# Up-projection of a decoder block by seven half-size products instead of eight, with the second pair's second product between the first pair's fifth and third

## What is computed

```
h = h + merged @ w_out
hn = rms_norm(h, ffn_norm_w)
up = causal_depthwise_conv(hn @ w_up, ffn_conv_w, ffn_conv_b)   # 3 taps
a, gt = split(up, 2)
h = h + (silu(gt) * a) @ w_down
```

## Time and profile before

| | us |
|---|---|
| median of 3 runs (2016.22 to 2018.52) | 2017.21 |
| the profiled execution's own time | 2021.11 |
| its span, first to last instruction | 2019.3 |
| TensorE busy | 1982.7 (98%) |
| VectorE busy | 953.9 (47%) |
| ScalarE busy | 673.2 (33%) |
| mean granted clock | 0.994 |

### The profile page before, as it was taken

One profiled execution on the slowest core, in us unless ns is written; L12 is line 12 of the kernel. 1 busy time (PEld: TensorE's weight loads), 2 busy tenths in 40 slices (PEclk: granted clock), 3 DMA queues, 4 the chain that ended last, 5 costly groups with the idle time before them and its releaser, 6 DMA issues.

```text
span 2019.3 us, 24049 instructions
## 1 busy us (share of the span) xinstructions
PE 1982.7 (98%) x9377; PEld 1698.6 (84%) x9377; DVE 953.9 (47%) x1199; ACT 673.2 (33%) x1179; POOL 98.4 (5%) x153
## 2 busy tenths in 40 slices
PE   6999999999999989999999999999999999999999
PEld 5888999999998877878887878788888888888887
DVE  5534532533443866995326252544344344343433
ACT  6323422432342254114325031433333323232232
POOL 1101110110100000001000010000000000000000
PEclk9999999999999998999999999999999999999999
DMA  6211211111122101210106132211112111022212
GB/s 239 95 52 38 71 61 42 47 50 42 42 69 100 42 1 42 63 42 22 63 22 189 43 113 96 105 42 42 42 46 79 42 42 42 10 84 88 94 47 73
DMA packets 84250, 129.24 MB, mean 64 GB/s; under 512 B 13705, under 2 KB 38281, under 8 KB 84169
## 3 DMA queue, kind: packets, MB, share of 16 engines
q1 hardware_dynamic: 76105, 117.53, 17.8%
q10 hardware_dynamic: 8064, 10.59, 1.5%
HBM read 111.20 MB, written 16.89 MB: 63 GB/s over the span
## 4 chain that ended last, share of the span: by engine, by line
PE 88%; DVE 7%; ACT 2%; DMA 1%; issue 1%; SPq 1%; POOL 0%; ACTq 0%; DVEq 0%
PE psum L248 28%; PE psum L250 28%; PE psum L249 28%; DVE acc L857 2%; DVE acc_odd L857 2%; PE psum L503 1%; DVE wlo L203 1%; PE psum L938 1%; PE psum L359 1%; ACT x_sc L997 1%; DMA x_rows<-in_x 1%; DVE softstat L1084 0%; DVE x_pt_lo L1093 0%; DMA grp<-group_out 0%; ACT x_sc L1012 0%
## 5 line engine op out<-in xcount | busy, mean ns | idle before, releaser
L248 PE MATMUL psum<-act_hi,wlo 128*128 128x512 f32 x1216 | 478.8, 394 | 1.3 <-DVE wlo L203 1.3
L250 PE MATMUL psum<-act_hi,whi 128*128 128x512 f32 x1216 | 474.6, 390 | 0.0
L249 PE MATMUL psum<-act_lo,whi 128*128 128x512 f32 x1216 | 474.5, 390 | 0.0
L248 PE MATMUL psum<-whi,act_lo 128*128 128x512 f32 x768 | 315.0, 410 | 3.0 <-DVE act_lo L1439 2.4
L250 PE MATMUL psum<-whi,act_hi 128*128 128x512 f32 x768 | 305.0, 397 | 0.0
L249 PE MATMUL psum<-wlo,act_hi 128*128 128x512 f32 x768 | 305.0, 397 | 0.0
L250 PEld LDWEIGHTS psum<-act_hi,whi 128*128 128x128 f32 x1216 | 228.9, 188 | 48.0
L248 PEld LDWEIGHTS psum<-act_hi,wlo 128*128 128x128 f32 x1216 | 229.1, 188 | 47.4 <-issue 1.4
L249 PEld LDWEIGHTS psum<-act_lo,whi 128*128 128x128 f32 x1216 | 229.1, 188 | 46.1
L198 ACT CAST whi<-stage 128x512 fp32r<-128x512 f32 x290 | 175.2, 621 | 256.7 <-PE psum L250 244.4
L203 DVE TENSOR_TENSOR wlo<-stage,whi 128x512 fp32r<-128x512 f32 x290 | 189.7, 688 | 118.8 <-ACT whi L198 117.9
(11 more groups left out here) (198 smaller groups left out, 2476.6 us busy)
## 6 DMA issues: line engine op xcount, KB each, us to landing
stage<-in_w_in SPq DMA_DIRECT2D x144, 256.0 KB, 4.1
stage<-in_w_up SPq DMA_DIRECT2D x88, 256.0 KB, 4.0
stage<-in_w_down SPq DMA_DIRECT2D x44, 256.0 KB, 2.6
group_out<-ob ACTq DMA_DIRECT2D x24, 256.0 KB, 2.1
grp<-group_out SPq DMA_DIRECT2D x24, 256.0 KB, 3.2
stage<-in_w_mem_kv SPq DMA_DIRECT2D x16, 256.0 KB, 8.7
x_rows<-in_x SPq DMA_DIRECT2D x2, 2048.0 KB, 13.5
stage<-in_w_out SPq DMA_DIRECT2D x16, 256.0 KB, 7.1
```

The costliest lines, as they stand in the source:

```text
L248: nc.tensor.matmul(dst, lhs[1], rhs[0], start=first, stop=False, skip_group_check=True)
L249: nc.tensor.matmul(dst, lhs[0], rhs[1], start=False, stop=False, skip_group_check=True)
L250: return nc.tensor.matmul(dst, lhs[0], rhs[0], start=False, stop=last, skip_group_check=True)
```

## The change

The up-projection of a pair is a 2 x 2 block product: gate and value columns by the two halves of the depth, and the two halves of the depth by the two halves of the tokens. The change computes it by Strassen's scheme in Winograd's form: 7 products of 4 depths x 512 tokens (12 matmuls each) instead of 8. Products 1, 2, 3 use plain blocks of weights or activations, the others use sums of them:

- Activations: four differences T1 to T4 of blocks, made once at the entry by VectorE from raw transposed rows `xt` (copied by ScalarE, no longer split from PSUM), then split like all operands (`t_act_hi`, `t_dve_lo`).
- Weights: for each pair four sums (`up_dve_sum`) on VectorE, seven high parts (`up_act_hi`) on ScalarE and seven low parts (`up_dve_lo`) on VectorE. The raw weights of a pair come by two DMAs of 512 KB (`up_load`).
- Results: products 1, 6, 5, 3 add into one PSUM bank, and ScalarE copies it between them (`s1`, `q1`, `q2`, `c12`); 2 has a bank, 7 and 4 share one. VectorE adds `c11`, `c22`, `c21` into `yg` and `yv` in SBUF; the taps are made from there.
- SBUF holds no `gated` any more during the stage: each pair's result goes to DRAM (`up_store`) and returns in `down_stage` (`load_gated`), pieces 8 to 21 first.
- TensorE's order in a pair is 6, 7, 5, then 1 of the next pair, 3, 4, then 2 of the next pair. At the entry: 1 and 2 of pair 0, 1 of pair 1 (from weights held in `u_next`), the last transposes, 6, 7, 5 of pair 0, 2 of pair 1, 3, 4. `u_next` lies on the bytes of `u_sums`. Batch 2 of the rows is transposed within tile 7 of `w_out_stage`.
- The first down pieces are split after the last pair is complete on both engines.

```diff
-N_UP = NU // 2
-BASE_DOWN = BASE_UP + N_UP * RING
+BASE_DOWN = BASE_UP
...
+        HALF_K = KT // 2
+        xt = [at(f"xt{b}", FREE + off, [KT, HB]) for b, off in enumerate((86016, 0, 8192, 16384))]
+        T_BYTES = HALF_K * CW * 4
+        t2, t3, t4 = ([at(f"t{n}_{part}", (2 * i + j) * T_BYTES, [HALF_K, CW], F32R)
...
+        moving = {1: b11, 2: b21, 3: b22, 4: t4, 5: t1, 6: t2, 7: t3}
...
+        u_raw = [at(f"u_raw{par}", U_W + par * 8192, [2, KT, P]) for par in range(2)]
+        u_hi = at("u_hi", U_W + 16384, [7, HALF_K, P], F32R)
+        u_lo = at("u_lo", U_W + 16384 + 14336, [7, HALF_K, P], F32R)
+        u_sums = at("u_sums", U_W + 45056, [4, HALF_K, P])
+        u_next = [at("u_next_hi", U_W + 45056, [2, HALF_K, P], F32R),
+                  at("u_next_lo", U_W + 45056 + 4096, [2, HALF_K, P], F32R)]
+        yg = at("yg", FREE, [S])
...
+        gated_dram = nc.dram_tensor("gated_scratch", (NU * P, S), F32).ap()
...
+        BANK_A, BANK_B, BANK_E = (0, 4), (1, 5), (2, 3)
...
+        H_PARTS = [(0, K1), (0, K2), (1, K1), (1, K2), (2, K2), (3, K2)]
+        def h_act_hi(act, which):
+            for n in which:
+                b, k = H_PARTS[n]
+                act.wait_ge(h_raw, (b + 1) * KT)
+                nc.scalar.copy(act_hi[:, k, h_cols(b)], xt[b][:, k, :]).then_inc(h_hi, 1)
...
+        T_SUMS = [(i, q) for q in range(2) for i in (1, 2, 3, 4)]
+        T_HALVES = [(2, 0), (3, 0), (1, 0), (4, 0), (2, 1), (3, 1), (1, 1), (4, 1)]
...
+            near, far = xt[q], xt[q + 2]
+            if i == 1:
+                dve.wait_ge(h_raw, (q + 3) * KT)
+                a, b = far[:, K1, :], near[:, K1, :]
+            elif i == 2:
+                dve.wait_ge(t_sum, T_SUMS.index((1, q)) + 1)
+                a, b = far[:, K2, :], t_raw(1, q)
+            elif i == 3:
+                a, b = far[:, K2, :], far[:, K1, :]
+            else:
+                dve.wait_ge(t_sum, T_SUMS.index((2, q)) + 1)
+                a, b = xt[q][:, K2, :], t_raw(2, q)
+            nc.vector.tensor_tensor(t_raw(i, q), a, b, ALU.subtract).then_inc(t_sum, 1)
...
+        up_cols = w_up.rearrange("(k p) (h c) -> p h k c", p=P, h=2)
+        def up_load(sp, U, par):
+            if not (isinstance(U, int) and U < 2):
+                sp.wait_ge(up_lo[4], U - 1)
+            for kind in range(2):
+                sp.dma_start(u_raw[par][:, kind], up_cols[:, kind, :, bass.ds(U * P, P)]).then_inc(raw_loaded[par], 16)
...
+        S_OF = {5: 0, 6: 1, 7: 2, 3: 3}
...
+        def up_act_hi(act, U, half_U, par, i, ahead=False):
+            first = isinstance(U, int) and U == 0
+            if i in S_OF:
+                act.wait_ge(up_sum, 4 * U + S_OF[i] + 1)
+            else:
+                act.wait_ge(raw_loaded[par], 32 * half_U + 32)
+            if ahead:
+                for n in S_OF:
+                    act.wait_ge(up_lo[n], 1)
+            elif not first:
+                act.wait_ge(up_p[i], U)
+            nc.scalar.copy(up_slot(i, 0, ahead), up_source(par, i)).then_inc(up_hi[i], 1)
...
+            if s == 0:
+                dve.wait_ge(raw_loaded[par], 32 * half_U + 32)
+                if isinstance(U, int) and U == 1:
+                    dve.wait_ge(up_p[1], 2)
+                    dve.wait_ge(up_p[2], 2)
+                ins = nc.vector.tensor_tensor(u_sums[:, 0], value_low, up_block(par, 4), ALU.add)
+            elif s == 1:
+                dve.wait_ge(up_sum, 4 * U + 1)
+                ins = nc.vector.tensor_tensor(u_sums[:, 1], u_sums[:, 0], up_block(par, 1), ALU.subtract)
+            elif s == 2:
+                ins = nc.vector.tensor_tensor(u_sums[:, 2], up_block(par, 1), value_low, ALU.subtract)
+            else:
+                dve.wait_ge(up_sum, 4 * U + 2)
+                ins = nc.vector.tensor_tensor(u_sums[:, 3], up_block(par, 2), u_sums[:, 1], ALU.subtract)
+            ins.then_inc(up_sum, 1)
...
+        def up_q2(act, U, par):
+            first = isinstance(U, int) and U == 0
+            act.wait_ge(up_p[5], U + 1)
+            if not first:
+                act.wait_ge(c22_done, U)
+            nc.scalar.copy(q2[:], psum[:, BANK_A[par], :]).then_inc(q2_done, 1)
...
+        def up_c22(dve, U, par):
+            dve.wait_ge(up_p[7], U + 1)
+            dve.wait_ge(q2_done, U + 1)
+            if not (isinstance(U, int) and U == 0):
+                dve.wait_ge(tap_v, 2 * U)
+            nc.vector.tensor_tensor(yv[:, N2], psum[:, BANK_E[par], :], q2[:], ALU.add).then_inc(c22_done, 1)
...
+        def up_mul(pe, U, par, i, ahead=False, between=None):
+            pe.wait_ge(up_lo[i], U + 1)
+            bank = (BANK_B if i == 2 else BANK_E if i in (7, 4) else BANK_A)[par]
+            for k in range(HALF_K):
+                mm = three(pe, psum[:, bank, :], [up_slot(i, part, ahead)[:, k, :] for part in range(2)],
+                           [half[:, k, :] for half in moving[i]], k == 0 and i in (1, 2, 7), k == HALF_K - 1)
+                if k == HALF_K - 1:
+                    mm.then_inc(up_p[i], 1)
+                if between:
+                    between(k)
...
+        def up_pe_3(pe, U, par):
+            pe.wait_ge(q2_done, U + 1)
+            up_mul(pe, U, par, 3)
...
+                        if j == 1 and t == 7:
+                            def between(k):
+                                if k == 4:
+                                    pe.wait_ge(row_scaled, hr.tile0 + 3 * H_BATCH)
+                                if k >= 4:
+                                    h_pe_bank(pe, 2, 2 * k - 8)
+                                    h_pe_bank(pe, 2, 2 * k - 7)
...
+            def middle(pe, U, par):
+                up_pe_6(pe, U, par)
+                up_pe_7(pe, U, par)
+                up_pe_5(pe, U, par)
+                up_pe_1(pe, U + 1, 1 - par)
+                up_pe_3(pe, U, par)
+                up_pe_4(pe, U, par)
+                up_pe_2(pe, U + 1, 1 - par)
...
+                pe.wait_ge(h_lo, 3)
+                up_pe_1(pe, 0, 0)
+                pe.wait_ge(gemm_freed, io + 2 * NT)
+                pe.wait_ge(h_lo, 4)
+                up_pe_2(pe, 0, 0)
+                pe.wait_ge(row_ss, hr.tile0 + NT)
+                up_pe_1(pe, 1, 1, True)
+                pe.wait_ge(row_scaled, hr.tile0 + NT)
+                for k in range(KT):
+                    h_pe_bank(pe, 3, k)
+                pe.wait_ge(t_lo, T_HALVES.index((2, 1)) + 1)
+                up_pe_6(pe, 0, 0)
+                pe.wait_ge(t_lo, T_HALVES.index((3, 1)) + 1)
+                up_pe_7(pe, 0, 0)
+                pe.wait_ge(t_lo, T_HALVES.index((1, 1)) + 1)
+                up_pe_5(pe, 0, 0)
+                up_pe_2(pe, 1, 1, True)
+                pe.wait_ge(h_lo, 6)
+                up_pe_3(pe, 0, 0)
+                pe.wait_ge(t_lo, T_HALVES.index((4, 1)) + 1)
+                up_pe_4(pe, 0, 0)
+                for U in (1, 2):
+                    middle(pe, U, U % 2)
+                with pe.Fori(1, NU // 2 - 1) as cc:
...
+            def pair_act(act, U, half_U, half_next, par):
+                np = 1 - par
+                start = isinstance(U, int) and U == 0
+                last = isinstance(U, int) and U == LAST
+                if not start:
+                    if not last:
+                        up_act_hi(act, U + 1, half_next, np, 1)
+                    up_silu(act, U - 1, np)
+                up_q1(act, U, par)
+                if not last:
+                    up_act_hi(act, U + 1, half_next, np, 6)
+                    up_act_hi(act, U + 1, half_next, np, 7)
+                up_q2(act, U, par)
+                if not last:
+                    if not start:
+                        up_act_hi(act, U + 1, half_next, np, 2)
+                    up_act_hi(act, U + 1, half_next, np, 5)
+                    up_s1(act, U + 1, np)
+                    up_act_hi(act, U + 1, half_next, np, 3)
+                up_c12(act, U, par)
+                up_base(act, 1, U, half_U, par)
+                if not last:
+                    up_act_hi(act, U + 1, half_next, np, 4)
+                up_base(act, 0, U, half_U, par)
+            def scalar(act):
+                t_act_hi(act, T_HALVES[1:4])
+                h_act_raw(act, 3)
+                up_s1(act, 0, 0)
+                t_act_hi(act, T_HALVES[4:7])
...
+            def pair_dve(dve, U, half_next, par):
+                np = 1 - par
+                start = isinstance(U, int) and U == 0
+                last = isinstance(U, int) and U == LAST
+                up_c11(dve, U, par)
+                if not start:
+                    if not last:
+                        up_dve_lo(dve, U + 1, np, 1)
+                    up_taps(dve, 0, U - 1, np)
+                    up_product(dve, U - 1, np)
+                if not last:
+                    up_dve_sum(dve, U + 1, half_next, np, 0)
+                    up_dve_sum(dve, U + 1, half_next, np, 1)
+                    up_dve_lo(dve, U + 1, np, 6)
```

(29 more changed lines are left out.)

576 lines of the change are left out of this document (356 added, 220 removed).

## The result

The changed kernel takes 2024.6 us (median of 10 runs, 2021.4 to 2029.4) where the kernel before takes 2019.3 in the same sitting (10 runs). One of those ten, at 2448.1 us, lies far off and is not in the ratio. The ratio is 1.0027, with a 95% interval of 1.0019 to 1.0035: 5.4 us slower. The forecast was 6.2 us slower. The profiled execution has a span of 2023.4 us, beside 2019.3 before.

A forecast was written before the change was run, and what follows sets the result against it. TensorE, 98% busy, bounds the old kernel; a VectorE-ScalarE round would bound the new loop. -59.7 + 23.2 + 25.4 - 0.9 + 10.7 + 7.5 = +6.2 us on the 2017.2 median: 2023, own range 2012 to 2036, with rivals 2003 to 2042.

The forecast's parts named there:

- Matmuls removed: Up-projection: 84 matmuls a pair instead of 96, 264 fewer in all at 0.2263 us each, -59.7 us if TensorE stays fed.
- last rival: Up-projection: products of t_hi and u_hi tiles cost TensorE another price than act and w tiles; 10 us either way, chance 0.02.
- the round is not 21 us: Rival, up-projection loop: the round takes 21.0 us or more, +12 or more, 2036; chance 0.10.
- the returning pieces: Rival, first half of the down-projection: eight gated pieces return late by 2 us each, +16, 2039; chance 0.06.
- The loop: Up-projection pairs: TensorE waits 1.3 us a pair before the third product in pairs 3 to 20, +23.2 us.
- The round: Up-projection: handovers between VectorE, ScalarE and TensorE from one third sum to the next, 20.35 us against TensorE's 19.01.
- second rival: Up-projection loop: TensorE bounds it after all, the +23.2 us vanish, 2000; chance of half that way (2011) or better 0.18.
- The entry: From tile 5 of w_out into the first pairs: waits in the three engines' queues leave TensorE idle, +25.4 us.
- The exit: First down-projection pieces: splits queue behind the last pair's work, 9.7 us, plus 1.0 at pair 21's third product; +10.7 us.
- The 0 for the spill of gated and its return: Down-projection: gated goes to DRAM and returns, 512 KB a piece asked for two pieces (10.9 us) ahead; cost 0.
- The clock: Five idle places outside the loop: each is followed by a fall of TensorE's clock, 5 x 1.5 = +7.5 us.
- Old entry idle, table loads, weight loads: Old entry's 0.9 us loss goes; lost table loads, hidden before, worth 0; 1 MB weight loads a pair, 0.

The follow-up runs named there:

- gs_high: The change with the high half of the down-projection's even-slot gated piece at byte 224,768 of each partition instead of 28,800; one run of 2028.9 us.
- q2_first: The change with ScalarE copying q2 ahead of the high half of sum 7 in every pair, instead of behind it; 2011.5 us, ratio 0.9960.
- q2_late: The change with ScalarE copying q2 behind two more high halves (2 and 5 of the next pair); 2046.8 us, ratio 1.0132.
- move_back: The change with the second product of pair 1 put back right behind the first product of pair 1; 2021.1 us, ratio 1.0012.
- p2_after_tr: The change with the second product of pair 1 right behind the last transposes, ahead of the first t_hi product; 2019.2 us, ratio 0.9999.
- entry_dve: The change with VectorE's additions, low halves and scaling of tiles 4 and 5 reordered at the end of w_out; 2016.6 us, ratio 0.9988.
- exit_all: exit_early, and SyncE also asks for the first two gated and w_down pieces before waiting to spill pair 20; 2014.2 us, ratio 0.9972.
- exit_early: The change with ScalarE's and VectorE's splits for the first two down-projection pieces moved ahead into the last pair; 2019.1 us, ratio 1.0000.
- align: The change with the up-projection's weight tiles and the one tile behind them 32 bytes further up in SBUF; 2025.4 us, ratio 1.0030.
- combined: The change with q2_first, exit_all, p2_after_tr and entry_dve together; 1990.2 us, ratio 0.9856.

## Why the prediction was right, point by point

Executions differ by some us before the up-projection begins (tile 5 of w_out starts at 1272.48 before and at 1269.90 in the changed kernel, in code that is the same), so I compare from there. From tile 5 to the first gs matmul it was 503.7 us and is 508.3: +4.5, forecast +4.7. The down-projection behind it takes 2.2 us longer, forecast 1.5. Together 6.7 against 6.2.

- **Matmuls removed: right in number, 264; their worth mis-sized.** The term took the old 0.2263 us for the new matmuls too. They take 0.234, and 22 x (21.72 - 84 x 0.234) is 45.4, not 59.7: 14.3 us less. The prediction had this as its last rival ("a product of t_hi and u_hi tiles costs TensorE another price", chance 0.02, 10 us either way) and set it aside because shapes are the same. The place is not, and gs_high shows that the place of a stationary operand alone is worth 3%. Its other rivals did not come true: the round is not 21 us, and the returning pieces were in time, since TensorE is busy for all of 1778.15 to 2019.
- **The loop: right, and the reason why most of the error above cost nothing.** The round was forecast at 20.35 and is 20.38. Step by step the rows of the round agree: gate base 1.16 (1.15), value base to the next high half 1.06 (1.07), gate base to gate tap 1.29 (1.30). Since the round, not TensorE, sets the pair, slower matmuls only fill the wait: 0.67 us of slower matmuls and 0.44 of recorded idle time (and what a restart costs) stand where the prediction had 1.34 of waiting. q2_first and q2_late show the round to be the cause, each to 0.05 us a pair. Against the 19.66 us that TensorE needs, the 17 pairs from 4 to 20 wait 0.72 us each: 12.2 us, where the term was 23.2. Had the prediction's second rival come true, its 2000 would have been about 2014, by the 14.3 us of slower matmuls.
- **The entry: 19.2 us of waiting instead of 25.4.** Place by place, with the forecast in brackets: 2.21 (2.7), 2.55 (3.0), transposes 0.5 (0.5; three waits of 0.16 at their weight loads), 6.52 (7.2), product 5 0.46 (0.8 and 2.3 for products 7 and 5), product 3 4.87 (5.0), then 1.71 and 0.37 (2.4, 0.9, 0.6). Most forecasts are a little over, probably in part because the walk's TensorE was 3% too fast and slower matmuls cover more of a wait; product 5's q1 wait was over-sized. move_back, p2_after_tr and entry_dve each moved the waits as the walk has them.
- **The exit: 9.42 and 0.68 (9.7 and 1.0).** Right in size and cause, as exit_all shows. The 0 for the spill of gated and its return held for the change, but only because SyncE's queue had time to spare; exit_early found it out.
- **The clock: right in place, short in size.** (1 - clock) over the windows above gives 1.7 + 1.7 + 2.4 + 3.0 + 2.5 = 11.3 us, where 5 x 1.5 = 7.5 was taken. The row it was taken from the earlier trace rows had a clock of 0.57 in its first 4 us and 1.00 in the next; behind the longer idle times it is 0.50 and then 0.74 to 0.90. Some of this varies from one execution to the next (move_back).
- **Old entry idle, table loads, weight loads: 0.9, 0, 0.** Nothing in the trace speaks against them; 512 KB of weights land in 5.1 us, twice a pair.

So the total is better than its parts. The matmuls' worth is 14.3 us short, and the loop's wait, 12.2 instead of 23.2, takes in 11.0 of it. That is no luck: a loop bound by a round takes in slower matmuls. The other 3.3 and the 3.8 of the clock stand against 6.2 that the entry's waits and 0.6 that the exit's are below the forecast. Slower matmuls shorten some of the entry's waits too, but that these remainders come out at 0.3 is luck.

What stays open: why a stationary operand high in SBUF slows even the matmul of the triple that doesn't use it, where in SBUF the step lies (the tiles that are fast end at 131,200, the slow ones begin at 134,624), and whether moving the up-projection's weights down would bring the spacing back to 0.2267 and pay once the round is shorter than 19.68; the room there is taken by the moving tiles.

## What to carry to other kernels

An engine that is 98% busy is a bound only until its work shrinks; before trusting the gain, walk one period through the fixed queues of the others, every queue that the data passes, the one that issues DMAs too. If that round is longer than the work left, the order of one copy in one queue is worth more than the arithmetic saved: here one line brought 13.5 us, and four such moves 34.5. A filler product belongs where TensorE waits for something that doesn't wait for the filler.

## What the hardware showed that I had not expected

- Spacing of 128x512 matmuls depends on where the operands lie in SBUF: 0.2267 us with both below byte 131,200 of the partition; 0.2337 with the stationary high half at 224,768, 0.2343 with the stationary weights at 183,776 and above (0.2328 with these 32 bytes further up, in align); 0.2289 with a moving one (in two of three matmuls) at 224,768. In the kernel before, the tile bact at 134,624 and above, moving in all three, has 0.2334, against 0.2268 for act. 3% over 1,848 matmuls is 14 us. Of these places only those at 224,768 were tried as the one thing changed.
- In the trace of before, the projections whose stationary tile takes every fourth token show 0.2350 us a matmul, those of the third group, with a wider stride, 0.2455, the plain ones 0.2270. No run here was made on it.
- The length of an idle time alone does not tell whether the clock falls. Before the fifth product of pair 1, idle times of 1.71, 1.96 and 2.04 us (the change, q2_late and entry_dve) left it at 1.00; 1.84 (align) and 1.86 (exit_early) were followed by 0.57, and 2.85 (combined) by 0.50. Before the third product of pair 0, 2.87 us left it at 1.00 (move_back), and 2.87 was followed by 0.57 (p2_after_tr). The 1.91 us of the earlier trace rows was followed by 0.57. Idle times of 0.44 and 1.47 us in each pair left it at 1.00.
